# Routed experts: activations stationary and 512 weight columns streaming in the down product, with three small changes of order

## The reference, cut to what matters

```python
def swiglu(h, w_gate, w_up, w_down):
    return (jax.nn.silu(h @ w_gate) * (h @ w_up)) @ w_down

# layer 0: w_gate, w_up 1024 x 2816, w_down 2816 x 1024
x = x + swiglu(hn, ffn_w_gate, ffn_w_up, ffn_w_down)
# layer 1: w_gate, w_up 8 x 1024 x 3584, w_down 8 x 3584 x 1024
logits = tokens @ router_w
top_vals, top_idx = lax.top_k(logits, 2)
combine = sum over the two of one_hot(top_idx) * softmax(top_vals)
for e in range(8):
    out = out + combine[:, e:e + 1] * swiglu(tokens, w_gate[e], w_up[e], w_down[e])
```

## Time and profile before

| what | value |
|---|---|
| median of 3 runs | 2055.0 us (2054.35 to 2058.61) |
| profiled execution, its own time | 2054.16 us |
| its span | 2052.4 us |
| TensorE busy / weight load busy | 1962.2 us (96%) / 1742.7 us (85%) |
| VectorE / ScalarE / GpSimd busy | 392.6 / 271.1 / 88.2 us |
| DMA | 482.92 MB, mean 235 GB/s |
| mean granted TensorE clock | 0.984 |

### The profile page before, as it was taken

One profiled execution on the slowest core, in us unless ns is written; L12 is line 12 of the kernel. 1 busy time (PEld: TensorE's weight loads), 2 busy tenths in 40 slices (PEclk: granted clock), 3 DMA queues, 4 the chain that ended last, 5 costly groups with the idle time before them and its releaser, 6 DMA issues.

```text
span 2052.4 us, 66808 instructions
## 1 busy us (share of the span) xinstructions
PE 1962.2 (96%) x31214; PEld 1742.7 (85%) x31214; DVE 392.6 (19%) x948; ACT 271.1 (13%) x579; POOL 88.2 (4%) x174
## 2 busy tenths in 40 slices
PE   7999999999999999999999799999999999999997
PEld 7888887888777788888788799999999898989896
DVE  3335331110000133533211300101000101010001
ACT  1223223000000122222320000000000000000001
POOL 4011101000000001011000000000000000000000
PEclk9999999999999999999999899999999999999999
DMA  7313123467442151311345389999999999999996
GB/s 239 123 44 102 43 84 103 144 207 244 144 144 82 42 160 47 101 45 43 107 139 204 137 335 407 407 407 407 407 407 407 407 407 407 407 407 407 407 407 240
DMA packets 214760, 482.92 MB, mean 235 GB/s; under 512 B 11582, under 2 KB 110092, under 8 KB 214668
## 3 DMA queue, kind: packets, MB, share of 16 engines
q1 hardware_dynamic: 214668, 481.54, 62.9%
HBM read 480.46 MB, written 1.05 MB: 235 GB/s over the span
## 4 chain that ended last, share of the span: by engine, by line
PE 83%; DMA 6%; SPq 4%; DVE 3%; ACT 1%; issue 1%; POOL 0%; DVEq 0%; POOLq 0%
PE bank L1190 29%; PE bank L623 18%; PE bank L1144 7%; DMA pool<-in_moe_w_down_dram 6%; PE bank L713 5%; PE bank L1071 4%; PE bank L1104 4%; SPq L2111 3%; PE bank L1087 3%; PE bank L636 2%; PE bank L677 2%; PE bank L1299 1%; SPq L2116 1%; PE bank L1034 1%; DVE pool L1814 0%
## 5 line engine op out<-in xcount | busy, mean ns | idle before, releaser
L1190 PE MATMUL bank<-pool 128*64 128x80 f32 x21504 | 759.5, 234 | 32.1 <-DMA pool<-in_moe_w_down_dram 23.5
L1190 PEld LDWEIGHTS bank<-pool 128*64 128x64 f32 x21504 | 752.6, 138 | 40.3 <-DMA pool<-in_moe_w_down_dram 25.8
L623 PE MATMUL bank<-hnT,pool 128*128 128x256 f32 x1856 | 431.5, 386 | 6.4 <-DVE pool L1876 6.4
L623 PEld LDWEIGHTS bank<-hnT,pool 128*128 128x128 f32 x1856 | 349.0, 192 | 61.7 <-issue 14.4
L1144 PEld LDWEIGHTS bank<-hnT,pool 128*128 128x128 f32 x640 | 121.6, 190 | 24.6 <-issue 9.1
L1144 PE MATMUL bank<-hnT,pool 128*128 128x256 f32 x640 | 141.2, 379 | 0.0
L2019 DVE TENSOR_TENSOR pool<-pool,bank 128x320 f32<-128x320 f32 x32 | 15.6, 488 | 637.4 <-ACT pool L1584 637.4
L713 PEld LDWEIGHTS bank<-pool 64*64 64x64 f32 x3008 | 94.8, 135 | 17.2 <-issue 11.3
L713 PE MATMUL bank<-pool 64*64 64x32 f32 (+2 forms) x3008 | 103.4, 221 | 2.6 <-DVE pool L1660 1.6
L1584 ACT ACTIVATE pool<-bank 128x320 f32<-128x320 f32 x32 | 14.0, 437 | 675.5 <-PE bank L1190 675.5
L561 POOL TENSOR_TENSOR pool<-pool,level_mask 128x256 f32<-128x256 f32 x72 | 51.9, 736 | 782.1 <-DVE pool L1736 502.1
(11 more groups left out here) (323 smaller groups left out, 1222.4 us busy)
## 6 DMA issues: line engine op xcount, KB each, us to landing
pool<-in_moe_w_up_dram SPq DMA_DIRECT2D x128, 896.0 KB, 16.6
pool<-in_moe_w_gate_dram SPq DMA_DIRECT2D x128, 896.0 KB, 16.6
pool<-in_w_in_dram SPq DMA_DIRECT2D x66, 1024.0 KB, 5.3
pool<-in_moe_w_down_dram SPq DMA_DIRECT2D x64, 1024.0 KB, 16.8
pool<-in_moe_w_down_dram SPq DMA_DIRECT2D x32, 1536.0 KB, 18.6
pool<-in_ffn_w_gate_dram SPq DMA_DIRECT2D x11, 1024.0 KB, 8.5
pool<-in_ffn_w_up_dram SPq DMA_DIRECT2D x11, 1024.0 KB, 5.7
pool<-in_ffn_w_down_dram SPq DMA_DIRECT2D x11, 1024.0 KB, 5.1
```

The source lines that it names most:

```text
L623: ins = mm(ps[:, s * T:(s + 1) * T], w[:, k, (j + s) * P:(j + s + 1) * P], hnT[:, k, :], start=(k == 0), stop=(k == KD - 1))
L1190: ins = mm(bank[rows, cs], w[:, rows], rhs, start=start, stop=stop, skip_group_check=True)
```

## The change

In the experts' down product the operands change places: a tile of heT (128 x 80) is the stationary operand and 512 columns of the down weights stream, so the result stands as 80 slots x 1024 features and goes to ye in one copy. The transposes, yT and its copies are gone. In the dense mixer six tiles are kept back instead of three. In attention the second group of gate pieces is four instead of five, and VectorE's copies are spread one to a pair of heads. At the start of a layer VectorE evicts half 0 before it normalises half 1.

```diff
@@ -110,7 +110,7 @@
         head_scalars = sb("head_scalars", [P, DEPTH, 2, GH])
         router_w = sb("router_w", [P, KD, NE])
         eps_c = sb("eps_c", [P, 4])
-        zeros = sb("zeros", [P, 4 * CAP], mybir.dt.bfloat16)
+        zeros = sb("zeros", [P, 512], mybir.dt.bfloat16)
         stat = sb("stat", [P, 64])
         sc = sb("sc", [P, 176])
@@ -1055,7 +1052,7 @@
                     some(steps, 5)
                     sums(2 * j)
                     sums(2 * j + 1)
-                    some(steps, 5)
+                    some(steps, 4)
                     values(j)
             def merge(l, steps):
@@ -1145,7 +1142,7 @@
                                          start=(k == 0), stop=(k == KD - 1))
                         ff_mm.by(ins)
-                        if f - 1 >= LAST - 2:
+                        if f - 1 >= LAST - 5:
                             kept.append(former)
                         else:
                             down_tile(*former)
@@ -1219,7 +1216,7 @@
                     pe.wait_ge(xg_ready, i * 2 + 2)
                     pe.wait_ge(selT_ready, i + 1)
                     for half in range(2):
-                        mm(B[4 + half][:, 0:4 * CAP], zeros[:, 0:P], zeros[:, :], start=True, stop=False,
+                        mm(B[4 + half][0:CAP, :], zeros[:, 0:CAP], zeros[:, :], start=True, stop=False,
                            skip_group_check=True)
                     with pe.Fori(0, NR) as j:
@@ -1271,10 +1268,9 @@
                             for half in range(2):
                                 for f in groups[g]:
                                     n, at = min(f // 2, 2), f - 2 * min(f // 2, 2)
-                                    for k in range(4 * half, 4 * half + 4):
-                                        ins = columns_mm(B[4 + half], slice(k % 4 * CAP, (k % 4 + 1) * CAP),
-                                                         down_slot(n)[:, at, k * P:(k + 1) * P], heT[:, f, :],
-                                                         start=False, stop=False)
+                                    ins = mm(B[4 + half][0:CAP, :], heT[:, f, :],
+                                             down_slot(n)[:, at, half * 512:half * 512 + 512], start=False, stop=False,
+                                             skip_group_check=True)
                                 if g == 1:
                                     ins.then_inc(dwn_mm, 1)
                                 elif half == 1:
@@ -1286,11 +1282,6 @@
                     pe.wait_ge(sc_added, i * 4 + 4)
                     gather(i + 1)
-                    for half in range(2):
-                        pe.wait_ge(yT_ready, i * 2 + (half + 1))
-                        for k in range(4):
-                            ins = pe.transpose(B[2 + half][0:CAP, k * P:(k + 1) * P], yT[:, 4 * half + k, :], ident[:])
-                        ins.then_inc(ye_mm, 1)
                     pe.wait_ge(xg_ready, i * 2 + 4)
                     for half in range(2):
                         for t in range(NT):
@@ -1589,11 +1580,7 @@
                 for half in range(2):
                     act.wait_ge(dwn_mm, i * (2 * NR) + (down_base + 2 * NR - 1 + half))
-                    A(yT[:, 4 * half:4 * half + 4, :], B[4 + half][:, 0:4 * CAP].rearrange("p (k n) -> p k n", k=4),
-                      ACT.Copy).then_inc(yT_ready, 1)
-                for half in range(2):
-                    act.wait_ge(ye_mm, i * 2 + (half + 1))
-                    A(ye[0:CAP, half * 512:half * 512 + 512], B[2 + half][0:CAP, :], ACT.Copy).then_inc(ye_ready, 1)
+                    A(ye[0:CAP, half * 512:half * 512 + 512], B[4 + half][0:CAP, :], ACT.Copy).then_inc(ye_ready, 1)
             ln_exp_tables()
             act.wait_ge(all_added, 1)
             for t in range(NT):
@@ -1858,7 +1845,7 @@
                                    B[3 + q][:, :].rearrange("p (s t) -> p s t", s=2), ALU.mult))
             def attention(l):
-                opens = ((), (0, 1), (2,), (3,))
+                opens = ((0,), (1,), (2,), (3,))
                 for j in range(4):
                     for h in (2 * j, 2 * j + 1):
                         l1_ready.wait(v, l, h + 1)
@@ -1909,7 +1896,7 @@
                     ff_silu.wait(v, 0, f + 1)
                     ff_ready.by(tt(ffT[:, f, :], sg[:, f % 2, 0:T], proj[f % 2][:, T:2 * T], ALU.mult))
                 for t in range(NT):
-                    down_mm.wait(v, 0, down_mm.per_layer - 2 * (1 - t))
+                    down_mm.wait(v, 0, down_mm.per_layer - 3 * (1 - t))
                     for half in range(2):
                         cs = slice(512 * half, 512 * half + 512)
                         ins = tt(x[:, t, cs], x[:, t, cs], B[2 * t + half][:, :], ALU.add)
@@ -2037,10 +2024,10 @@
                 scaled(l, 0, 0)
                 v.wait_ge(vec_mm, l + 1)
                 v.tensor_copy(vecs[:, l, 0:V_ROWS], proj[1][:, 0:V_ROWS]).then_inc(vec_ready, 1)
+                v.wait_ge(vec_ready, l + 1)
+                turned(l, 0, 0)
                 scaled(l, 0, 1)
-                v.wait_ge(vec_ready, l + 1)
-                for t in range(NT):
-                    turned(l, 0, t)
+                turned(l, 0, 1)
                 lerps = lerp_steps(l)
                 deltanet(l, lerps)
                 rwkv(l, lerps)
```

More of the change, by code:

```diff
@@ L222, in build @@
         heT = region(FB * CAP).rearrange("p (j n) -> p j n", j=FB)
-        yT = region(KD * CAP).rearrange("p (k n) -> p k n", k=KD)
         sge = region(FB * CAP).rearrange("p (j n) -> p j n", j=FB)
@@ L437, in build @@
         he_silu, he_ready, hid_mm, dwn_mm = ff_silu.handle, ff_ready.handle, proj_mm.handle, down_mm.handle
-        yT_ready = sem("yT_ready")
-        ye_mm = sem("ye_mm")
         ye_ready = sem("ye_ready")
```

## The result

The changed kernel takes 2142.89 us (median of 4 runs, 2142.22 to 2143.11) against 2056.11 us (4 runs, 2054.35 to 2058.61): ratio 1.0421, 95% interval 1.0403 to 1.0439. It is 87 us slower; the forecast was 2142.

A forecast was written before the change was run, and what follows sets the result against it. The experts were taken as bound by the weight stream, TensorE having under 6 us of slack a pass. +96.9 - 9.0 - 1.2 = +86.7 us on 2054.16 gave 2140.9, stated as 2142, range 2128 to 2162.

The forecast's parts named there:

- The down product: Experts' down product: 28 records of 0.43 us, 12.04 us a round, replace 224 records taking 7.78 us.
- The bound changes sides: Experts: TensorE, at 27.78 us a round, becomes slower than the weight stream at 26.98 us; no wait added.
- that rival: Experts: TensorE still waits for weights 5.75 us in seven passes, 40 us more, 2182 us; chance 5%.
- the rival in which the stream stays the bound: Experts: the weight stream still sets the pass at 107.9 us, giving 2044 us; chance 3%.
- Weight loads: Rival, down product: loads of 80 columns don't hide behind the matmul ahead, 124 us more, 2266 us; chance 3%.
- The changes of form: Experts' round: two changes between array halves and whole array add 0.2 us, bounds nothing and 0.4.
- The end of a pass: Experts, between passes: transposes and their copy wait go, scatter starts 0.7 us sooner; the end is 8.2 us.
- The experts' sum: All expert passes: first pass grows 17.8 us, seven more 79.8, last end saves 0.7; +96.9 us.
- Attention: Attention, two layers: VectorE's copy comes earlier, saving TensorE's wait and half clock; gain 9.0 us, bounds 5 and 10.
- Start of a layer: First projection: evictions of half 0 no longer wait behind a normalisation; gain 0.6 us a layer, 1.2 in all.
- Six tiles: Dense mixer: the earlier half 0 is not what VectorE's normalisation waits for; counted as 0.
- The total: Whole kernel: +86.7 us against the profiled 2054.16 gives 2140.9; forecast median 2142 us.

The follow-up runs named there:

- the pair with 64 columns: Changed kernel with 64 of 80 activation columns stationary: both feature halves on the same partitions, 2133.17 us; halves alternating on different partitions, 2043.06 us.

## Why the prediction was right, point by point

**The down product.** I took 0.43 us a record from the dense down tiles and had 12.04 us plus 0.2 for changes of form. Measured are 0.429, with the change of form apart, and a round of 27.82 against 27.78. The reason given, 80 of 128 columns filled and nothing beside, is shown by the pair with 64 columns. The rule on the issue gap in the Trainium skill (TensorE: Matmul & The Clock Gate, Back-to-back issue gap), 131 ns at 512 columns, does not hold for these float32 records, which stand 0.429 us apart.

**The bound changes sides.** Shown by the pair with shorter down loads: 39 us in the kernel before, nothing in the changed one. No wait for weights came in, so that rival falls, and with it the rival in which the stream stays the bound.

**Weight loads.** They stay hidden: the pace is the same with 64 and with 80 columns in the load.

**The changes of form.** Mis-sized a little: 0.31 us a round, where 0.2 was taken. Over 32 rounds that would be 3.5 us more, but the rounds came out only 0.04 us longer than forecast, 1.3 us in all. The other terms were a little too high: hidden() without a change of form takes 15.49 us, not 448 x 34.7 ns = 15.54, and the records 12.01, not 12.04.

**The end of a pass.** Predicted 8.2 us, measured 1414.15 - 1405.69 = 8.46. TensorE took up the scatter 1408.79 - 1405.69 = 3.10 us after the gather's start, 3.0 were worked out. Another 0.12 us is the opening of the banks with 512 columns, 1414.15 - 1413.60 = 0.55 against 0.43; it was named in the prediction but left out of its sum.

**The experts' sum.** +96.9 predicted, 99.35 - 0.55 = +98.8 in the trace. Seven passes came out 0.4 us longer each than forecast, 119.74 against 119.3. Against that the first pass took 1.4 us less, 1285.95 - 1172.20 = 113.75 where 97.4 + 17.8 = 115.2 were forecast.

**Attention.** -9.0 predicted; 5.0 us in each layer, 10.0 in all, in every trace that has the edit (layer 0 of the changed kernel from 1.81 us behind to 3.19 ahead), and 10.6 between the medians. The residual wait was 0.22 instead of 0.4, and no half clock followed. The wait and the half clock make 4.7 of the 5.0 us; the other 0.3 is not placed.

**Start of a layer.** The first projection did come 0.86 us earlier in layer 0 and 0.54 in layer 1 of the changed kernel, 1.4 in all. In the time of the kernel 1.2 us isn't shown: the interval of the run alone reaches 1.8 us either way.

**Six tiles.** 0 predicted, 0 found, for the reason given.

**The total.** The mechanisms are right. That the median was hit within 1 us is partly luck. The experts cost 1.9 us more than predicted, and attention gave 1.0 us more. The clock also took part: between the first projection and the instruction at 91.11 (L791 before, L788 after) the changed kernel lost 2.7 us in layer 0, and between the same instructions of layer 1 it won 2.5 us back. The last section shows that this stretch varies by as much without any edit.

## What to carry to other kernels

When two operands can change places, count the part of the array that each form fills and what may run beside it, and then the records times their pace; fewer and longer instructions weren't cheaper here, where the weight loads were hidden in both forms. Where two bounds lie 5% apart, the first part of an edit's cost only uses up the slack, and the rest is paid in full, so work out both sides in the same unit (us a round). A copy that stands behind work which is waiting for something else is a cheap gain, here 10 us for an edit of two lines, and a third of that was the half clock after the wait.

## What the runs showed that I had not expected

Up to 90 us the kernel before and the run with attention alone issue the same instructions, and so does the one with the exchange alone apart from the size of the zeros. Yet the instruction that starts at 91.11 in the first starts at 93.77 and 94.54 in the others. The mean clock from 76 to 92 was 0.89, 0.79 and 0.69 (before, attention alone, exchange alone):

```profile
76.00:92.00 16.00, 16.00 (x93) 0.89 0.21 66
```

```profile
76.00:92.00 16.00, 16.00 (x87) 0.79 0.21 66
```

```profile
76.00:92.00 16.00, 16.00 (x81) 0.69 0.21 66
```

In that stretch TensorE runs 32 matmul records of one column each (L768). Whether they are what lets the clock fall is not shown. How far it falls there varies between executions of the same code, and the starts lie 3.4 us apart, more than the layer-start edit can bring.

The run with the layer-start edit alone was to tell whether the edit moves the clock's dips. There the same instruction starts at 92.66, 1.55 us behind the kernel before, with a mean clock of 0.79. By the test as I wrote it this would say that the edit moves the dips and costs time here. The other traces don't support that. The kernel before with the kept tiles alone, without the edit, has 93.13, and with the shorter down loads 93.75. Over all traces the five without the edit lie between 91.11 and 94.54 and the seven with it between 92.36 and 93.73. The trace of the kernel before is the one early case, so the 1.8 us lie within what executions without the edit differ by. A test on one pair of traces can't settle such a question. The gain of 3.0 us around the start of layer 1 has the same fault: 2.5 us of it lie in the same stretch of layer 1.
